# One overflow block of a mixture of experts computed on the weights of place 15, with a place table written by the routing

## The chip, the cores and the metric

The kernel runs on one core of one Trainium2 chip. The core has a matrix engine (PE, with its weight loads as PEld), a vector engine (DVE), a scalar engine (ACT), a general engine (POOL), and a sequencer for transfers (SP). Sixteen DMA engines move data between device memory and the on-chip memory. The metric is the device time of one execution in microseconds (us).

## The reference, cut to what matters

The program is one layer of a trunk: four token mixers, a cross attention, and then a mixture of experts over 512 tokens. Only the last part is touched.

```python
def _hier_moe(h, w_group, b_group, w_router, b_router, w1, w3, w2):
    g_sel = argmax(t @ w_group + b_group)            # 4 groups
    top_p, top_i = top_k(softmax(e_logits[rows, g_sel]), 2)
    expert = g_sel[:, None] * 8 + top_i              # 32 experts, two per token
    def expert_block(args):
        xb, e = args
        hid = silu(xb @ w1[e]) * (xb @ w3[e])        # 1024 -> 512
        return hid @ w2[e]                           # 512 -> 1024
    out = segment_sum(ys * slot_w[:, None], slot_tok)
```

512 tokens with two experts each make 1,024 rows, which fall on 32 experts. All is float32. The weights of one expert are three matrices of 1024x512, 6.29 MB. The reference draws its inputs from a fixed seed. Counted with its own routing they put 65 rows on expert 21 and at most 54 on any other.

## The kernel before

**Stages.** Up to about 806 us of the profiled execution the mixers and the cross attention run. Then comes the normalisation and the routing (the block from L1537), and from about 849 us the experts (the block from L1818 on each engine). The last stage adds the experts' rows to the tokens, normalises, and stores the result.

**An expert's turn.** Every expert gets one turn of up to `FIRST` = 64 rows. POOL gathers the rows from `xn_scratch` with an indirect DMA (`fetch`, L1869). PE turns them over (`e_x`, L1786), ACT copies them (`xT`). PE multiplies them by the two up matrices (`up_half`, `e_u`, L1801: 32 matmuls in two halves of 16). ACT and DVE form the hidden rows, PE turns those over (`e_h`, L1792) and multiplies them by the down matrix (`down_half`, `e_y`, L1811: 16 matmuls). ACT copies the result, and POOL scatters it to `ys_scratch` (`store`, L1876). PE does `up(q)`, then the rows of turn q+1, then the hidden rows and the down part of turn q-1.

**Weights.** An expert's weights come in six pieces of 1 MiB (n = 0 to 3 the halves of w1 and w3, n = 4 and 5 those of w2), issued by SP (`load_piece`, L1515). There are 18 slots `w_raw`, three experts' worth. `AT` gives each piece a place in the order, and its place modulo 18 is its slot. The order is (0,0..3), (1,0..3), (0,4), (0,5), (2,0..3), (1,4), (1,5) and so on: each expert's up pieces stand ahead of the down pieces of the one before. Twelve pieces are issued during the routing (`EARLY_SLOTS`) and six more as the expert block begins. From there `ring` waits for each piece until the piece that held its slot before is used (`consumed`, on `s_used`), and issues the load. SP issues strictly in this order.

**Overflow.** An expert with more than 64 rows has its rest in further blocks of 64, each an overflow job. DVE works out a table of the jobs (`jobs`, L2073 to L2086). SP writes it to device memory with a small DMA (L1823), and each engine later reads the number of jobs from there (TENSOR_LOAD). The experts run in two halves of `MID` = 16. Between them stands a loop over the jobs, on every engine. Its weights are six pieces loaded again (L1841), into slots that the order leaves open between the halves (`OVER`). The loop's rows come through `list_scratch`: POOL reads the job's row list (`ibl`, L1891), DVE makes the indices (`job_ids`), POOL gathers `xo` (L1895). At the end of each pass POOL stores the result, waits for it, and fetches list and rows of a next job, which may be empty. With the inputs above there is one job.

Of the kernel before, what the change touches and what calls it, by code (L numbers as in the profile page):

```python
# [23 lines left out]
U32 = mybir.dt.uint32  # L24
# [5 lines left out]
P = 128  # L30
# [26 lines left out]
ROUTE_CONSTS = 3 * P + EXPERTS + 3 * EXPERTS * BLOCKS + 2  # L57
# [7 lines left out]
JOBS = 16  # L65
LIST_UNIT = 16
# [36 lines left out]
def trunk(nc, a, out):  # L103
    stack = ExitStack()
    with stack:
# [1406 lines left out]
        def load_piece(sp, e, n):  # L1512
            j = AT[e, n] % DEPTH
# [13 lines left out]
        act_b, rank = (sbuf(stack, n, [P, EXPERTS * BLOCKS]) for n in ("act_b", "rank"))  # L1527
        ones_b = sbuf(stack, "ones_b", [P, EXPERTS * BLOCKS])
# [5 lines left out]
        blk_thr, blk_at, blk_e = (rc[:, r0 + EXPERTS * BLOCKS * i:r0 + EXPERTS * BLOCKS * (i + 1)] for i in range(3))  # L1534
        r0 += 3 * EXPERTS * BLOCKS
        rank1, half_no = rc[:, r0:r0 + 1], rc[:, r0 + 1:r0 + 2]
        with ExitStack() as c:  # L1537
# [6 lines left out]
            def load_gain(sp):  # L1544
# [4 lines left out]
                for j in range(EARLY_SLOTS):  # L1549
                    load_piece(sp, *ORDER[j])  # L1550
# [24 lines left out]
            idf = sbuf(c, "idf", [P, EXPERTS])  # L1575
# [150 lines left out]
        with ExitStack() as c:  # L1726
# [7 lines left out]
            ib2 = sbuf(c, "ib2", [P, 1])  # L1734
            xo, yoo = sbuf(c, "xo", [FIRST, D]), sbuf(c, "yoo", [P, FF])
# [15 lines left out]
            s_turn, o_zero = sem("o_turn"), sem("o_zero")  # L1751
            LAST = EXPERTS - 1
# [14 lines left out]

            def slot(q, n):
                return SLOT[q, n]

            def landed(eng, q, n):
                eng.wait_ge(s_raw[slot(q, n)], 16 * (len(IN_SLOT[q, n]) + 1))

            def consumed(eng, q, n):
                if q >= 0:
                    eng.wait_ge(s_used[slot(q, n)], len(IN_SLOT[q, n]) + 1)

            def y_of(t, ch):
                return raw[slot(*END[t])][:, ch * D:(ch + 1) * D]

            junk = raw[slot(*END[T])][:, 0:D]
            final_gain = raw[slot(*END[T])][:, D:2 * D]
# [36 lines left out]
            def _(sp):  # L1819
                for piece in ORDER[EARLY_SLOTS:DEPTH]:  # L1820
                    load_piece(sp, *piece)
                sp.wait_ge(s_jobs, 1)
                sp.dma_start(jobs_dram[0:1, 0:4 * (JOBS + 1)].rearrange("o (j q) -> (o j) q", q=4),  # L1823
                             jobsi[0:JOBS + 1, :]).then_inc(s_jobs_out, 16)
                def ring(pieces):
                    for e, n in pieces:
                        consumed(sp, *IN_SLOT[e, n][-1])
                        load_piece(sp, e, n)

                ring(FIRST_HALF[DEPTH:])  # L1830
                sp.wait_ge(s_jobs_out, 16)
                n = sp.value_load(jobs_dram[0:1, 2:3], min_val=0, max_val=MAX_EXTRA)
                with sp.If(n > 0):
                    for piece in FIRST_HALF[OVER_AT - DEPTH:][:PIECES]:
                        consumed(sp, *piece)
                    with sp.Fori(0, n) as r:
                        e = sp.value_load(jobs_dram[0:1, bass.ds(r * 4 + 1, 1)], min_val=0, max_val=EXPERTS - 1)
# [9 lines left out]
                for piece in END:  # L1847
                    consumed(sp, *piece)
                sp.dma_start(final_gain, bass.AP(a["rows"].tensor, 0, [[0, P], [1, D]])).then_inc(f_gain, 16)
                for b in range(2):  # L1850
                    sp.wait_ge(s_ys[b], 16 * (EXPERTS // 2))
# [10 lines left out]
            def _(pool):  # L1862
# [3 lines left out]
                def fetch(q):  # L1866
                    b = q % 2
                    wait(pool, s_tx, q - 1)
                    pool.indirect_dma_start(xs[b][:], None, xn_dram,  # L1869
                                            bass.IndirectOffsetOnAxis(idx[0:FIRST, q:q + 1], 0),  # L1870
                                            bounds_check=last_x, oob_is_err=False).then_inc(s_xs[b], 16)

                def store(q):
                    b = q % 2
                    pool.wait_ge(s_yo, q + 1)
                    pool.indirect_dma_start(ys_halves, bass.IndirectOffsetOnAxis(idy[:, q:q + 1], 0),  # L1876
                                            yo[b][:], None,
# [21 lines left out]
                for q in range(MID):  # L1899
# [3 lines left out]
                    if q == LIST_AT:  # L1903
                        pool.wait_ge(s_scattered, 16 * 2 * T)
                        pool.wait_ge(s_jobs_out, 16)
                        list_of(0)
                    if q == LIST_AT + 2:
                        pool.wait_ge(s_ids, 2)
                        pool.wait_ge(o_zero, 1)
                        rows_of_job()  # L1910
                store(MID - 1)
                n = pool.value_load(jobs_dram[0:1, 2:3], min_val=0, max_val=MAX_EXTRA)
                with pool.If(n > 0):
                    with pool.Fori(0, n) as r:
                        pool.wait_ge(o_yo, r + 1)
# [6 lines left out]
                        list_of(r + 1)  # L1922
                        pool.wait_ge(s_ids, r * 2 + 4)
                        pool.sem_inc(s_turn, 1)
                        rows_of_job()
                    pool.nop()
                pool.wait_ge(o_xs, n * 16 + 16)
                pool.sem_inc(s_turn, 1)
                for q in range(MID, EXPERTS):
                    if q + 2 < EXPERTS:  # L1930
                        fetch(q + 2)
                    if q > MID:
                        store(q - 1)
                store(LAST)
                for b in range(2):
                    pool.wait_ge(s_ys[b], 16 * (EXPERTS // 2))

            @block.tensor
            def _(pe):
# [5 lines left out]
                def up(q):  # L1945
                    pe.wait_ge(s_xT, q + 1)
                    wait(pe, s_hd, q - 1)
                    for half, (n1, n3) in enumerate(((W1A, W3A), (W1B, W3B))):
# [3 lines left out]
                        m1.then_inc(s_used[slot(q, n1)], 1)  # L1952
                        m3.then_inc(s_used[slot(q, n3)], 1)
# [6 lines left out]
                def down(q):  # L1960
                    pe.wait_ge(s_hT, q + 1)
                    wait(pe, s_yo, q - 1)
                    for half, n in enumerate((W2A, W2B)):
                        landed(pe, q, n)
                        down_half(half, q % 2, q % 2, slot(q, n)).then_inc(s_used[slot(q, n)], 1)
# [14 lines left out]
                experts(0, MID)  # L1980
                pe.wait_ge(s_jobs_out, 16)
                n = pe.value_load(jobs_dram[0:1, 2:3], min_val=0, max_val=MAX_EXTRA)
                with pe.If(n > 0):
                    pe.wait_ge(s_yo, MID)
# [21 lines left out]
                experts(MID, EXPERTS)  # L2006

            @block.scalar
            def _(act):
# [35 lines left out]
                experts(0, MID)  # L2045
                act.wait_ge(s_jobs_out, 16)
# [13 lines left out]
                experts(MID, EXPERTS)  # L2060
                consumed(act, *END[T])
# [7 lines left out]
            def _(dve):  # L2069
                do = Steps(dve, s_dve)  # L2070

                thr = blk_thr.rearrange("p (e b) -> p e b", b=BLOCKS)
# [174 lines left out]
```

## Time and profile before

| what | value |
|---|---|
| median of 3 runs | 1394.78 us (1394.43 to 1395.49) |
| the profiled execution, its own time | 1392.87 us |
| its span in the profile | 1390.9 us |
| PE busy | 1207.1 us, 87% of the span |
| DVE, ACT, POOL busy | 528.9, 407.6, 95.8 us |
| DMA, mean over the whole span | 217 GB/s |
| loads of weight pieces (`w_raw<-in_w`) | 198 (192 of the experts, 6 of the job) |

The busy shares are means over stages with different limits. From about 807 us on, the experts' weights stream in, and the rate of the DMA engines has to be read for that stretch alone.

### The profile page before, as it was taken

The numbers are of one execution on the slowest core, as the hardware profiler recorded it, in microseconds if no ns is written. First come the engines' busy times: TensorE is split into PE (matmuls) and PEld (weight loads), VectorE is DVE, ScalarE is ACT, GpSimd is POOL, SyncE is SP. The second block draws the span as 40 slices with busy tenths as digits, with TensorE's granted clock in tenths as the row PEclk, the third lists the DMA queues.
The fourth block names the chain that finished last, engine by engine and source line by source line (L and its number), as shares of the span: only waits on it lengthen the run. The fifth ranks groups of instructions, "written<-read, shape, count | busy, mean of one in ns | idle before, by whom it ended". The sixth has DMA issues, their size and how long they took to land. (4 is left out here: it accounts for less than half of the span.)

```text
span 1390.9 us, 15072 instructions
## 1 busy us (share of the span) xinstructions
PE 1207.1 (87%) x6038; PEld 795.0 (57%) x6038; DVE 528.9 (38%) x934; ACT 407.6 (29%) x674; POOL 95.8 (7%) x125
## 2 busy tenths in 40 slices
PE   6999999999999999999997854999777749977781
PEld 5887877777688787888886632333333213333330
DVE  4334464767857368555356434111000001100014
ACT  6234442444443342243153130122111101211112
POOL 2000000000000000000000003111111011111100
PEclk9999999999999999999999985999999979999996
DMA  7313213121123222423221079999999999999995
GB/s 270 116 63 105 77 63 132 49 88 57 46 70 112 76 84 91 174 91 114 100 113 61 0 310 318 374 408 405 415 417 407 426 403 402 406 414 415 407 397 196
DMA packets 50599, 301.63 MB, mean 217 GB/s; under 512 B 8985, under 2 KB 9385, under 8 KB 20451
## 3 DMA queue, kind: packets, MB, share of 16 engines
q1 hardware_dynamic: 41778, 281.06, 51.9%
q0 software_dynamic: 8224, 17.52, 3.7%
q10 hardware_dynamic: 528, 2.10, 0.4%
q8 instruction: 48, 0.79, 0.2%
q14 instruction: 21, 0.16, 0.0%
HBM read 296.77 MB, written 12.93 MB: 223 GB/s over the span
## 5 line engine op out<-in xcount | busy, mean ns | idle before, releaser
L1801 PE MATMUL e_u<-w_raw,xT 128*64 128x512 f32 x1056 | 240.4, 601 | 54.8 <-DMA w_raw<-in_w 51.3
L1801 PEld LDWEIGHTS e_u<-w_raw,xT 128*64 128x64 f32 x1056 | 80.1, 138 | 209.6 <-issue 205.5
L2092 DVE SCALAR_TENSOR_TENSOR tn<-tn,e_u 64x512 f32<-64x512 f32 x32 | 21.7, 679 | 413.3 <-ACT tn L2023 413.3
L296 DVE TENSOR_TENSOR s_lo<-s_raw,s_hi 128x2048 fp32r<-128x2048 f32 (+1 forms) x68 | 138.5, 2037 | 55.2 <-ACT s_hi L291 54.6
L291 ACT CAST s_hi<-s_raw 128x2048 fp32r<-128x2048 f32 (+1 forms) x68 | 115.9, 1704 | 110.2 <-PE pz L547 41.1
L1811 PE MATMUL e_y<-w_raw,hidT 128*64 128x512 f32 x528 | 125.1, 617 | 15.4 <-ACT hidT L2018 15.0
L515 PE MATMUL pz<-hT_hi,s_hi 128*128 128x512 f32 x288 | 116.4, 404 | 0.0
L515 PE MATMUL pz<-hT_hi,s_lo 128*128 128x512 f32 x288 | 112.7, 391 | 0.0
L515 PE MATMUL pz<-hT_lo,s_hi 128*128 128x512 f32 x288 | 112.6, 391 | 0.0
L2013 ACT COPY xT<-e_x 128x512 f32<-128x512 f32 x32 | 18.8, 586 | 312.9 <-PE e_x L1786 312.9
L531 PE MATMUL pz<-hT_hi,s_hi 128*128 128x512 f32 x256 | 102.2, 399 | 0.5
L531 PE MATMUL pz<-hT_lo,s_hi 128*128 128x512 f32 x256 | 99.7, 389 | 0.0
L531 PE MATMUL pz<-hT_hi,s_lo 128*128 128x512 f32 x256 | 99.7, 389 | 0.0
L1811 PEld LDWEIGHTS e_y<-w_raw,hidT 128*64 128x64 f32 x528 | 36.0, 140 | 79.8 <-issue 59.8
L547 PE MATMUL pz<-zR,s_hi 128*128 128x512 f32 x192 | 63.0, 389 | 0.0
L515 PEld LDWEIGHTS pz<-hT_hi,s_hi 128*128 128x128 f32 x288 | 54.4, 189 | 13.8 <-issue 3.3
L1786 PEld LDWEIGHTS e_x<-ident,xs 64*128 64x128 f32 x256 | 30.7, 200 | 53.5 <-DMA xs<-xn_scratch,idx 27.9
L515 PEld LDWEIGHTS pz<-hT_lo,s_hi 128*128 128x128 f32 x288 | 54.3, 189 | 11.8
L515 PEld LDWEIGHTS pz<-hT_hi,s_lo 128*128 128x128 f32 x288 | 54.5, 189 | 10.1
L1786 PE MATMUL e_x<-ident,xs 64*128 64x64 f32 x256 | 35.1, 279 | 28.1 <-DMA xs<-xn_scratch,idx 26.9
L1876 POOL DMA_INDIRECT ys_scratch<-yo,idy x32 | 32.2, 1006 | 377.4 <-ACT yo L2030 377.4
L948 ACT ACTIVATE tg<-pz 128x512 f32<-128x512 f32 x32 | 19.2, 598 | 125.6 <-PE pz L531 125.6
(357 smaller groups left out, 1897.0 us busy)
## 6 DMA issues: line engine op xcount, KB each, us to landing
w_raw<-in_w SPq DMA_DIRECT2D x198, 1024.0 KB, 28.0
s_raw<-in_w_mix SPq DMA_DIRECT2D x30, 1024.0 KB, 4.9
s_raw<-in_w_gb SPq DMA_DIRECT2D x32, 768.0 KB, 4.3
s_raw<-in_w_out_pieces SPq DMA_DIRECT2D x4, 1024.0 KB, 4.8
w_raw<-ys_scratch SPq DMA_DIRECT2D x8, 512.0 KB, 7.6
x_sb<-in_x SPq DMA_DIRECT2D x4, 512.0 KB, 4.9
rel_bias<-in_rel_tiles POOLq DMA_DIRECT2D x8, 256.0 KB, 3.1
decay<-in_decay POOLq DMA_DIRECT2D x8, 256.0 KB, 4.5
```

The costliest lines, as they stand in the source:

```text
L291: nc.scalar.copy(w_hi[n % 2][:, 0:w], w_raw[n % 2][:, 0:w]).then_inc(w_himade, 1)
L296: nc.vector.tensor_tensor(w_lo[n % 2][:, 0:w], w_raw[n % 2][:, 0:w], w_hi[n % 2][:, 0:w].bitcast(F32), ALU.subtract).then_inc(w_split, 1)
L515: last = nc.tensor.matmul(pz[j][:], wp, hp, start=(k == 0 and m == 0), stop=(k == KD - 1 and m == 2))
L531: last = nc.tensor.matmul(pz[0][:], wp, hp, start=(k == 0 and m == 0), stop=(k == KD - 1 and m == 2))
L547: last = nc.tensor.matmul(pz[1][:], wp, yp[:, k, :], start=(k == 0 and m == 0), stop=(k == KB - 1 and m == 2))
L948: nc.scalar.activation(tg[u % 2][:], pz[0][:], ACT.Tanh, scale=0.5).then_inc(g_tanh, 1)
L1786: last = nc.tensor.transpose(ps_x[:, k * FIRST:(k + 1) * FIRST], x[:, k::KD], ident[0:FIRST, 0:FIRST])
L1801: m = nc.tensor.matmul(ps_u[o][lo:lo + FIRST, :], xT[b][:, k * FIRST:(k + 1) * FIRST], raw[j][:, kk * FF:(kk + 1) * FF], start=k == 0, sto ...
L1811: m = nc.tensor.matmul(ps_y[o][lo:lo + FIRST, :], hT[b][:, k * FIRST:(k + 1) * FIRST], raw[j][:, kk * D + h * FF:kk * D + (h + 1) * FF], s ...
L1876: pool.indirect_dma_start(ys_halves, bass.IndirectOffsetOnAxis(idy[:, q:q + 1], 0), yo[b][:], None, bounds_check=last_y, oob_is_err=False) ...
L2013: nc.scalar.copy(xT[q % 2][:], ps_x[:]).then_inc(s_xT, 1)
L2092: nc.vector.scalar_tensor_tensor(tn[:], tn[:], 1.0, ps_u[b][0:FIRST, :], ALU.add, ALU.mult).then_inc(s_hm, 1)
```

## The change

Place 15's weights are used for two turns in a row: turn 15 for the first 64 rows, and a new turn 16 (`JOB`) for the first overflow job. There are now 33 turns. `weights_of(q)` maps a turn to a place. So that this is right for whichever expert overflows, that expert changes places with 15 (`PARTNER`). DVE writes a table `perm` of 32 entries, the expert at each place, behind the table of jobs. SP loads the weights of the places from 4 on (`FIXED` = 4) by an expert number that it reads from the table. The row indices of the places are swapped in the same way (`idx2`, `idy2`). Experts 0 to 3 are loaded before the table is there and can't be swapped: their blocks stand last in the list of jobs, and are run by the loop in the middle, as are all jobs beyond the first. If no other expert overflows, turn 16 runs on an empty list.

```diff
+            def weights_of(q):
+                return q - (q >= JOB)
...
             def consumed(eng, q, n):
-                if q >= 0:
-                    eng.wait_ge(s_used[slot(q, n)], len(IN_SLOT[q, n]) + 1)
+                if q == JOB - 1:
+                    eng.wait_ge(s_kept[n], 1)
+                elif q >= 0:
+                    freed(eng, weights_of(q), n)
+
+            def signal_of(q, n):
+                return s_kept[n] if q == JOB - 1 else s_used[slot(q, n)]
...
                 sp.wait_ge(s_jobs, 1)
                 sp.dma_start(jobs_dram[0:1, 0:4 * (JOBS + 1)].rearrange("o (j q) -> (o j) q", q=4),
                              jobsi[0:JOBS + 1, :]).then_inc(s_jobs_out, 16)
+                sp.dma_start(jobs_dram[0:1, PERM_AT:PERM_AT + EXPERTS], permi[0:1, :]).then_inc(s_jobs_out, 16)
+                sp.wait_ge(s_jobs_out, 32)
+                loaded = {q: q for q in range(FIXED)}
+
                 def ring(pieces):
-                    for e, n in pieces:
-                        consumed(sp, *IN_SLOT[e, n][-1])
-                        load_piece(sp, e, n)
+                    for q, n in pieces:
+                        if q not in loaded:
+                            loaded[q] = sp.value_load(jobs_dram[0:1, PERM_AT + q:PERM_AT + q + 1],
+                                                      min_val=0, max_val=EXPERTS - 1)
+                        freed(sp, *IN_SLOT[q, n][-1])
+                        load_piece(sp, q, n, loaded[q])
 
                 ring(FIRST_HALF[DEPTH:])
-                sp.wait_ge(s_jobs_out, 16)
...
-                for q in range(MID):
+                for q in range(JOB + 1):
                     fetch(q + 2)
...
-                experts(0, MID)
-                pe.wait_ge(s_jobs_out, 16)
+                experts(0, JOB + 1)
+                pe.wait_ge(s_jobs_out, 32)
                 n = pe.value_load(jobs_dram[0:1, 2:3], min_val=0, max_val=MAX_EXTRA)
...
-                do.after(nc.vector.tensor_copy(jobs[:, 2:3], rank[:, EXPERTS * BLOCKS - 1:EXPERTS * BLOCKS]))
+                do.after(nc.vector.tensor_scalar(jobs[:, 2:3], rank[:, JOB_BLOCKS - 1:JOB_BLOCKS], -1.0, None, ALU.add))
...
-                nc.vector.tensor_copy(jobsi[:], jobs[:]).then_inc(s_jobs, 1)
+                do.after(nc.vector.tensor_copy(jobsi[:], jobs[:]))
+
+                do.after(nc.vector.tensor_scalar(here[:], iota, e_of_job[:], None, ALU.is_equal))
+                do.after(nc.vector.tensor_scalar(gap[:], e_of_job[:], -1.0, float(PARTNER), ALU.mult, ALU.add))
+                do.after(nc.vector.scalar_tensor_tensor(perm[:], here[:], gap[:], iota, ALU.mult, ALU.add))
+                do.after(nc.vector.tensor_copy(perm[:, PARTNER:PARTNER + 1], e_of_job[:]))
+                nc.vector.tensor_copy(permi[:], perm[:]).then_inc(s_jobs, 1)
```

How the instructions stand: on SP's queue, at the start of the expert block, the kernel before has this. `jobs_scratch` is the device memory of the tables, `w_raw<-in_w` a piece of weights.

```order
20 L1515 DMA w_raw<-in_w 128x2048 x6
21 L1823 DMA jobs_scratch<-jobsi 17x4
22 L1515 DMA w_raw<-in_w 128x2048 x78
23 L1832 TENSOR_LOAD jobs_scratch
24 L1832 ISA x2
25 L1833 COMPARE_AND_BRANCH
```

The changed kernel has this in the same place.

```order
20 L1520 DMA w_raw<-in_w 128x2048 x6
21 L1845 DMA jobs_scratch<-jobsi 17x4
22 L1847 DMA jobs_scratch<-permi 1x32
23 L1520 DMA w_raw<-in_w 128x2048 x4
24 L1854 TENSOR_LOAD jobs_scratch
25 L1854 ISA x2
26 L1520 ISA
27 L1520 DMA w_raw<-in_w 128x2048 x2
28 L1520 ISA
29 L1520 DMA w_raw<-in_w 128x2048 x4
```

A second small DMA is behind the first, and from place 4 on a read of the table stands ahead of each place's first piece. The wait for both small DMAs is on the first piece of row 23.

On PE, at the end of the first half, the kernel before has this (`e_u` up, `e_h` hidden rows, `e_y` down, `e_x` rows; `xo` is the job's rows).

```order
3453 L1811 MATMUL e_y<-w_raw,hidT 64x512 x8
3454 L1801 MATMUL e_u<-w_raw,xT 64x512 x16
3455 L1792 MATMUL e_h<-ident,hd 128x64 x4
3456 L1811 MATMUL e_y<-w_raw,hidT 64x512 x8
3457 L1792 MATMUL e_h<-ident,hd 128x64 x4
3458 L1811 MATMUL e_y<-w_raw,hidT 64x512 x8
3459 L1982 TENSOR_LOAD jobs_scratch
```

The changed kernel has this.

```order
3454 L1823 MATMUL e_u<-w_raw,xT 64x512 x16
3455 L1808 MATMUL e_x<-ident,xs 128x64 x8
3456 L1814 MATMUL e_h<-ident,hd 128x64 x4
3457 L1833 MATMUL e_y<-w_raw,hidT 64x512 x8
3458 L1823 MATMUL e_u<-w_raw,xT 64x512 x16
3459 L1814 MATMUL e_h<-ident,hd 128x64 x4
3460 L1833 MATMUL e_y<-w_raw,hidT 64x512 x8
3461 L1814 MATMUL e_h<-ident,hd 128x64 x4
3462 L1833 MATMUL e_y<-w_raw,hidT 64x512 x8
3463 L2015 TENSOR_LOAD jobs_scratch
```

The rows, the up part and the down part of turn 16 stand between turn 15 and the read of the number of jobs. The loop behind that read is still there on every engine.

## Rows read from the trace of the kernel before

**Rows 1.** The page, parts 2 and 6: DMA by slice, and the weight loads (issue to landing).

```profile
DMA  7313213121123222423221079999999999999995
...
w_raw<-in_w SPq DMA_DIRECT2D x198, 1024.0 KB, 28.0
```

**Rows 2.** Stretches: start and end, length, granted TensorE clock, DMA share, GB/s.

```profile
940.00:1060.00 120.00, 1.00 1.01 412
1080.00:1100.00 20.00, 1.00 1.01 425
```

**Rows 3.** The page, part 4: the chain that ended last, by line, shares of the span.

```profile
SPq L1515 21%; PE e_u L1801 4%; DMA w_raw<-in_w 4%; PE e_y L1811 2%; DMA xs<-xn_scratch,idx 1%; DMA xo<-xn_scratch,ibx 1%; DVE x_sb L2135 1%; PE e_x L1786 1%; DMA ys_scratch<-yoo,iby 0%; DMA ibl<-list_scratch 0%; SPq L1841 0%; DVE x_sb L2129 0%; DMA w_raw<-ys_scratch 0%; PE e_h L1792 0%; POOLq L1888 0%
```

**Rows 4.** Timeline of SP, expert stage: start, length, line, operation, count.

```profile
853.56 0.31 SPq L1823 DMA_DIRECT2D jobs_scratch<-jobsi  x1
866.31 193.51 SPq L1515 DMA_DIRECT2D w_raw<-in_w  x78
1064.29 12.42 SPq L1841 DMA_DIRECT2D w_raw<-in_w  x6
1076.95 258.47 SPq L1515 DMA_DIRECT2D w_raw<-in_w  x96
```

**Rows 5.** Stretches at the start of the expert stage, columns as in rows 2.

```profile
849.00:850.00 1.00, 0.50 0.03 8
850.00:851.00 1.00, 0.50 0.93 115
851.00:852.00 1.00, 0.50 0.74 287
...
849.00:866.00 17.00, 0.51 0.96 287
866.00:877.00 11.00, 1.00 0.98 257
877.00:880.00 3.00, 1.00 0.99 356
```

**Rows 6.** SP's weight issues, 866.0 to 866.8: lengths in ns, starts, us to landing.

```profile
L1515 SPq DMA_DIRECT2D w_raw<-in_w x2: 353/529/705, 866.3 to 866.7; - x2
...
DMA to landing us min/median/max: 13.9/14.8/15.7
```

**Rows 7.** DMA queues from 845 to 885: POOL's gathers and scatters (packets, MB, share).

```profile
q0 software_dynamic: 576, 0.60, 5.4%
```

**Rows 8.** Timeline of DVE: a 32-wide operation, two 256-wide ones, turn 0's first.

```profile
848.01 0.18 DVE L1721 TENSOR_SCALAR second<-idf 128x32 f32<-128x32 f32 x1
...
851.17 0.35 DVE L2080 TENSOR_SCALAR rank<-rank,rc 128x256 f32<-128x256 f32 x1
851.56 0.48 DVE L2081 CUSTOM_DVE_ANT_0 act_b<-rank,rc 128x256 f32<-128x256 f32 x1
...
871.88 0.68 DVE L2092 SCALAR_TENSOR_TENSOR tn<-tn,e_u 64x512 f32<-64x512 f32 x1 [18.35 <-ACT tn L2023]
```

**Rows 9.** SP's table read and weight issues by line: ns min/median/max, starts.

```profile
L1832 SPq TENSOR_LOAD <-jobs_scratch x1: 712/712/712, 1059.9 to 1059.9; - x1
...
L1841 SPq DMA_DIRECT2D w_raw<-in_w x6: 362/2253/2531, 1064.3 to 1074.4; - x6
...
L1515 SPq DMA_DIRECT2D w_raw<-in_w x192: 327/2132/4704, 808.2 to 1333.3; - x192
```

**Rows 10.** Timeline of PE: turn 0's up part, turns 14 and 15, then turn 16.

```profile
859.66 10.05 PE L1801 MATMUL e_u<-w_raw,xT 128*64 128x512 f32 x32 [0.68 <-ACT xT L2013]
...
1076.17 3.65 PE L1801 MATMUL e_u<-w_raw,xT 128*64 128x512 f32 x16 [1.56 <-DMA w_raw<-in_w]
...
1080.91 3.65 PE L1811 MATMUL e_y<-w_raw,hidT 128*64 128x512 f32 x16 [0.46 <-ACT hidT L2018]
...
1112.33 7.09 PE L1801 MATMUL e_u<-w_raw,xT 128*64 128x512 f32 x32 [0.68 <-ACT xT L2013]
1119.35 1.09 PE L1786 MATMUL e_x<-ident,xs 64*128 64x64 f32 x8
```

More of the change, by code:

```diff
@@ L56 @@
 BLOCKS = 8
-ROUTE_CONSTS = 3 * P + EXPERTS + 3 * EXPERTS * BLOCKS + 2
+FIXED = 4
+PARTNER = EXPERTS // 2 - 1
+FREE_BLOCKS = (EXPERTS - FIXED) * BLOCKS
+JOB_BLOCKS = EXPERTS * BLOCKS + 1
+ROUTE_CONSTS = 3 * P + EXPERTS + 3 * JOB_BLOCKS + 2
 SMALL = 3 * KD + 8 * KB
@@ L1526, in trunk @@
         cnt = sbuf(stack, "cnt", [P, EXPERTS])
-        act_b, rank = (sbuf(stack, n, [P, EXPERTS * BLOCKS]) for n in ("act_b", "rank"))
-        ones_b = sbuf(stack, "ones_b", [P, EXPERTS * BLOCKS])
+        act_b, rank = (sbuf(stack, n, [P, JOB_BLOCKS]) for n in ("act_b", "rank"))
+        ones_b = sbuf(stack, "ones_b", [P, JOB_BLOCKS])
+        idf, idx2, idy2 = sbuf(stack, "idf", [P, EXPERTS]), *(
+            sbuf(stack, n, [P, EXPERTS], U32) for n in ("idx2", "idy2"))
         jobs, jobsi = sbuf(stack, "jobs", [P, 4]), sbuf(stack, "jobsi", [P, 4], I32)
@@ L1533, in trunk @@
         r0 += P
-        blk_thr, blk_at, blk_e = (rc[:, r0 + EXPERTS * BLOCKS * i:r0 + EXPERTS * BLOCKS * (i + 1)] for i in range(3))
-        r0 += 3 * EXPERTS * BLOCKS
+        blk_thr, blk_at, blk_e = (rc[:, r0 + JOB_BLOCKS * i:r0 + JOB_BLOCKS * (i + 1)] for i in range(3))
+        r0 += 3 * JOB_BLOCKS
         rank1, half_no = rc[:, r0:r0 + 1], rc[:, r0 + 1:r0 + 2]
@@ L1734, in trunk @@
             ib2 = sbuf(c, "ib2", [P, 1])
+            e_of_job, gap, here = (sbuf(c, n, [P, k]) for n, k in (("e_of_job", 1), ("gap", 1), ("here", EXPERTS)))
+            perm, permi = sbuf(c, "perm", [P, EXPERTS]), sbuf(c, "permi", [P, EXPERTS], I32)
             xo, yoo = sbuf(c, "xo", [FIRST, D]), sbuf(c, "yoo", [P, FF])
@@ L1750, in trunk @@
             last_x, last_y = nc.gpsimd.alloc_register("last_x"), nc.gpsimd.alloc_register("last_y")
-            s_turn, o_zero = sem("o_turn"), sem("o_zero")
-            LAST = EXPERTS - 1
+            s_turn, o_zero, s_swap = sem("o_turn"), sem("o_zero"), sem("swapped")
+            s_kept = [sem(f"kept{n}") for n in range(PIECES)]
+            JOB = MID
+            TURNS = EXPERTS + 1
+            LAST = TURNS - 1
             LIST_AT = MID // 2
@@ L1820, in _ @@
                 for piece in ORDER[EARLY_SLOTS:DEPTH]:
-                    load_piece(sp, *piece)
+                    load_piece(sp, *piece, piece[0])
                 sp.wait_ge(s_jobs, 1)
@@ L1921, in _ @@
                         pool.sem_inc(s_turn, 1)
[L1922 to L1925, printed above, removed]
                     pool.nop()
[L1927 to L1930, printed above, removed]
+                for q in range(JOB + 1, TURNS):
+                    if q + 2 < TURNS:
                         fetch(q + 2)
-                    if q > MID:
+                    if q > JOB + 1:
                         store(q - 1)
@@ L1964, in down @@
                         landed(pe, q, n)
-                        down_half(half, q % 2, q % 2, slot(q, n)).then_inc(s_used[slot(q, n)], 1)
+                        down_half(half, q % 2, q % 2, slot(q, n)).then_inc(signal_of(q, n), 1)
                 def experts(lo, hi):
@@ L2085, in _ @@
                 do.after(nc.vector.memset(jobs[:, 3:4], 0.0))
-                nc.vector.tensor_copy(jobsi[:], jobs[:]).then_inc(s_jobs, 1)
+                do.after(nc.vector.tensor_copy(jobsi[:], jobs[:]))
[4 more added lines that the diff above has]
+                nc.vector.tensor_copy(permi[:], perm[:]).then_inc(s_jobs, 1)
+                do.after(nc.vector.tensor_tensor_reduce(av[:, 0:EXPERTS], idf[:], here[:], 1.0, 0.0, ALU.mult, ALU.add,
+                                                        e_of_job[:]))
+                do.after(nc.vector.tensor_tensor(gap[:], idf[:, PARTNER:PARTNER + 1], e_of_job[:], ALU.subtract))
+                do.after(nc.vector.scalar_tensor_tensor(idf[:], here[:], gap[:], idf[:], ALU.mult, ALU.add))
+                do.after(nc.vector.tensor_copy(idf[:, PARTNER:PARTNER + 1], e_of_job[:]))
+                do.after(nc.vector.tensor_scalar(idy2[:], idf[:], 2.0, half_no, ALU.mult, ALU.add))
+                do.after(nc.vector.tensor_scalar(here[:], idf[:], float(N), -float(N), ALU.is_ge, ALU.mult))
+                nc.vector.tensor_tensor(idx2[:], idf[:], here[:], ALU.add).then_inc(s_swap, 1)
                 def experts(lo, hi):
```

113 lines of the change are left out of this document (68 added, 45 removed).

## Prediction

> **What bounds the kernel now.** I first look at the DMA row of the page. In the last third of the span, from about 860 us on, the 16 DMA engines are busy in full until the last slices [rows 1]. Averages over the whole span hide this. By stretch, the engines move 412 GB/s over 120 us of the first half and 425 GB/s where few gathers run [rows 2]. The chain that ended last says the same: its largest part is SP's issue of the weights, at 21% of the span [rows 3]. An issue on SP takes 0.33 us when nothing holds it, but 2.1 us in the median, and a piece lands 28 us after it [rows 9, 1]. One piece of 1.05 MB at 425 GB/s takes 2.47 us, so about 11 pieces are in flight and SP is held back by the full queue. PE needs 3.65 us for each half of an up part, and waits for a landing before it [rows 10]. So what ends last is the stream of 198 pieces. PE, idle for part of each turn, can take on a turn for nothing as long as the slots come free before the stream runs dry.
>
> **The change part by part.**
>
> *Six loads go.* The job's weights were six pieces between the halves [rows 4]. The inputs put 65 rows on expert 21, so there is one job, it falls to turn 16, and the loop's six loads are skipped. 6 x 1.049 = 6.29 MB. At 425 GB/s this is 14.8 us, at 412 GB/s, which has the gathers in it, 15.3 us. The gathers and the scatter of the job itself stay, and only one empty gather goes. I take 15.0 us, between the two.
>
> *DVE makes the second table.* New ahead of the signal to SP are one 257-wide comparison and one 257-wide reduction (0.35 and 0.48 us in the rows of their 256-wide kin), a reduction and four small operations in place of two (about 0.8 us together), and five 32-wide ones of 0.2 us. The sum is some 2.7 us [rows 8]. SP's small DMA stood at 853.6 [rows 4], and so moves to about 856.3, with the second one 0.4 us behind. Some seven more operations for the row indices end near 858.5. DVE's next work is at 871.9 [rows 8], so all of that is hidden.
>
> *SP waits for both tables before the ring.* This is the term that costs. In the kernel before, the ring's first pieces are issued at 866.3, as PE sets the slots free [rows 4, 6]. Now SP must first see the tables landed, and they are queued behind the six pieces issued at 849 to 852. When does the last of those land? From 849 to 866 the engines move 17 x 0.287 = 4.88 MB, to 877 another 2.83 MB, to 880 another 1.07 MB: 8.78 MB [rows 5]. Of this 0.60 MB is gathers and scatters [rows 7], so 8.2 MB are weights, and 1.9 MB of them are ring pieces. The earliest end of the six is where 6.29 + 0.6 MB are moved, at 873.8. The latest is one piece (2.5 us) ahead of the first ring piece's landing, 866.3 + 13.9 = 880.2 [rows 6], so 877.7. Give the tables 0.4 us more: the ring starts between 874.2 and 878.1. A stream starting from nothing loses 1.7 us on top: in its first 3 us after 849 it moved 0.41 MB, less the 0.3 us before the first issue, where 2.7 us at 425 GB/s are 1.15 MB [rows 5]. By 880 the ring has then moved 1.7 MB in the early case and 0.1 MB in the late one, against 1.9 MB. The lost 0.2 to 1.8 MB are 0.4 to 4.3 us of a stream that is full from there to the end, so nothing gives them back. I take 3.0 us, nearer the late end, since the landing at 880.2 is a row and the early end is only a sum of bytes. PE isn't held up: its up weights of turns 0 to 2 are among the first 18 pieces.
>
> The Trainium skill (DMA: Bandwidth & Descriptors, Anatomy of one DMA) puts about 2 us of fixed cost on a DMA, most of it the receipt of the write from the target memory. By that price, in place of my 0.4 us, the ring would start 1.6 us later, the term would be 4.6 us and the time 1384.4. No row here gives a landing of the small DMA.
>
> *SP reads the table 28 times.* One read takes 0.71 us and some register work [rows 9], about 1 us in all, per place of six pieces or 15 us. SP otherwise sits 2.1 us in each issue because the queue is full. A pause of 1 us leaves some 10 pieces in flight instead of 11: nothing, as long as SP is not the bound. The issues with an address from a register took 0.36 us at the least, as good as those with a constant [rows 9].
>
> *The turn in the middle.* Place 15's up slots come free a turn later. Turn 15's second up half starts at 1076.2 [rows 10]. Behind it in the queue are then the down pieces of places 14 and 15 and the up pieces of 16, eight pieces or 19.7 us, to 1095.9. The six slots left open in the order help only later, since they stand behind in SP's order. PE goes on with 3.65 us of up, 1.1 us of rows, 1.2 us for the hidden rows, 3.65 us of down, and half of turn 16's up part, 3.5 us [rows 10]: the first kept slots are free at 1089.3, 6.6 us before the stream would end, or 5 us with the start loss. So I cost the kept slots at nothing. If that cover were gone, each microsecond beyond it would be one of time. The loop's own waits go too, but the stream ran on at full rate beside them [rows 2], so they bring nothing.
>
> *Sum.* -15.0 + 3.0 = -12.0 us. Against the profiled execution, 1392.87 us, this is 1380.9. The median of the runs is 1.9 us above that execution, and I carry the difference over: 1394.78 - 12.0 = 1382.8 us. The case's own range, from 14.8 to 15.3 and 0.4 to 4.3, is 1379.9 to 1384.3.
>
> **The rivals.**
>
> *The tables come early (A).* If the small DMAs don't queue behind the weights, SP is back at the ring by 866 and the second term is nothing: 1379.8. For it speaks that they go to other memory and are tiny. Against it speaks that ring pieces on this queue land in the order of their issue, 14 to 16 us later with a short queue [rows 6].
>
> *The stream runs dry in the middle (B).* The cover is 5 us at full clock. Turn 0's up part took 10.05 us where the granted clock was 0.50 for most of it, against 7.09 in the middle [rows 10, 5]. If PE's clock is low around turns 15 and 16, the 9.5 us from 1079.8 to 1089.3 grow to as much as 19, the stream stands still for about 4.5 us, and the second pair of slots adds a little: some 5 us, 1387.8. Against it: the granted clock was 1.00 in 1080 to 1100 [rows 2].
>
> *SP becomes the bound, slower (C).* The 2.1 us median of an issue may be the making of a piece's transfers, and not a wait for room. Then SP has no slack, and each of the 28 reads stands in full in the stream: 28 x 1.0 = 28 us, and 1410.8. The point from which this decides is 12.0 / 28 = 0.43 us uncovered in each read. Against it: the issues of 0.33 to 0.53 us at the ring's start [rows 6, 9], when the queue was short.
>
> *The change doesn't do what it says (D).* If the expert that overflows were one of the fixed four, or had two blocks, the loop would load its six pieces as before: 1394.8 + 3.0 = 1397.8. The count of rows speaks against it.
>
> **How the numbers follow.** A measurement of this kernel can tell about 0.2%, 2.8 us, from no change. Forecast 0.66, A 0.12, B 0.14, C 0.04, D 0.02, and 0.02 for smaller sizes of B and C that end near the old time. Faster is the sum of the first three, 0.92. Same is 0.02, slower 0.06. The predicted time is the forecast's, 1382.8. The range takes in A, the forecast with the bounds of both terms, and B with something to spare: 1378.5 to 1389.0. C and D lie outside.
>
> **What would show it.** 192 weight loads in place of 198, and none from the loop. SP's first ring issue at 874 to 878 in place of 866, and a dip of the DMA rate between 870 and 880. From there on 410 to 425 GB/s without a gap, also around 1090. The read of the table on SP 28 times at 0.7 us, with the next issue shorter by about as much. DVE's chain some 2.7 us longer ahead of the first small DMA. The last expert's up part about 12 us earlier than in the kernel before, and the stage behind it unchanged. The forecast is wrong if the first ring issue is before 870 (A), if the DMA share falls near the middle (B), or if landings drift apart from 28 us down to a few while SP is the one busy (C).

## The result, and the profile after

| | time |
|---|---|
| the kernel before, same chip | 1394.61 us median (1394.40 to 1395.49, 4 runs) |
| the changed kernel | 1382.28 us median (1379.14 to 1385.35, 4 runs) |
| ratio | 0.991, 95% interval 0.9887 to 0.9933 |
| the profiled execution of the changed kernel | 1379.14 us, span 1377.2 us |

The change takes off 12.3 us where 12.0 were forecast, and 1382.28 stands beside the forecast's 1382.8. The profiled execution is the fastest of the four, so its own gain on the profiled execution before is larger, 13.7 us.

The page of the changed kernel, parts 2 and 6, with the lines that answer to [rows 1]:

```profile
DMA  7323213212123222433322059999999999999995
...
w_raw<-in_w SPq DMA_DIRECT2D x192, 1024.0 KB, 28.2
```

There are 192 loads in place of 198, and a piece still lands 28 us after its issue: the stream is full and is still the bound. The timeline of SP in the expert stage (start, length, line, operation, count), to be held against [rows 4]:

```profile
849.38 3.06 SPq L1520 DMA_DIRECT2D w_raw<-in_w  x6
857.18 0.30 SPq L1845 DMA_DIRECT2D jobs_scratch<-jobsi  x1
857.53 0.23 SPq L1847 DMA_DIRECT2D jobs_scratch<-permi  x1
876.59 445.94 SPq L1520 DMA_DIRECT2D w_raw<-in_w  x174
```

The small DMA is issued at 857.2 in place of 853.6, and the ring begins at 876.6 in place of 866.3. Between them the DMA engines run out of work. By stretch (start and end, length, granted clock, DMA share, GB/s), changed kernel:

```profile
874.00:875.00 1.00, 1.00 1.08 295
875.00:876.00 1.00, 1.00 0.57 173
876.00:877.00 1.00, 1.00 0.15 37
877.00:878.00 1.00, 1.00 1.01 115
878.00:879.00 1.00, 1.00 0.45 156
879.00:880.00 1.00, 1.00 0.96 401
...
849.00:866.00 17.00, 0.51 0.95 272
866.00:877.00 11.00, 1.00 0.87 207
877.00:880.00 3.00, 1.00 0.81 224
880.00:900.00 20.00, 1.00 1.01 417
```

Against [rows 5], 17 x 0.015 + 11 x 0.050 + 3 x 0.132 = 1.2 MB are missing by 880, 2.8 us of the stream at 425 GB/s. That is the term of 3.0 us, read from this trace.

In the middle, PE's timeline of the changed kernel shows turn 16 with no wait for a landing ahead of its up part:

```profile
1077.72 3.65 PE L1823 MATMUL e_u<-w_raw,xT 128*64 128x512 f32 x16 [1.21 <-DMA w_raw<-in_w]
...
1083.35 3.65 PE L1833 MATMUL e_y<-w_raw,hidT 128*64 128x512 f32 x16 [0.47 <-ACT hidT L2051]
1086.83 7.04 PE L1823 MATMUL e_u<-w_raw,xT 128*64 128x512 f32 x32
...
1336.40 3.65 PE L1823 MATMUL e_u<-w_raw,xT 128*64 128x512 f32 x16 [1.29 <-DMA w_raw<-in_w]
```

The first and the last of these rows give a ruler for all the kernels here. From turn 15's second up half to the last expert's it is 1336.40 - 1077.72 = 258.7 us. In the kernel before it is 1349.90 - 1076.17 = 273.7 us, the end of it from this row of the trace of before:

```profile
1349.90 3.65 PE L1801 MATMUL e_u<-w_raw,xT 128*64 128x512 f32 x16 [1.30 <-DMA w_raw<-in_w]
```

So the later part, in which the bytes of the six loads were moved, is 15.0 us shorter. The earlier part, from the issue of the six pieces to turn 15, is 228.3 us in place of 226.9. That is 1.4 us more, where the count of bytes gave 2.8. The next section shows that this earlier part differs by more than that between executions of the same code, so it can't decide between the two.

### The profile page after: what moved, and what is told of

Read it like the earlier page. It is cut to its first block and busy times, and to the rows that moved or that the text cites. A ratio compares the mean times of both kernels' runs of the same rounds, so it can differ in the third digit from the quotient of the medians.

```text
span 1377.2 us, 15337 instructions
## 1 busy us (share of the span) xinstructions
PE 1207.4 (88%) x6038; PEld 796.1 (58%) x6038; DVE 533.0 (39%) x950; ACT 407.4 (30%) x674; POOL 92.7 (7%) x122
## 5 line engine op out<-in xcount | busy, mean ns | idle before, releaser
L1823 PE MATMUL e_u<-w_raw,xT 128*64 128x512 f32 x1056 | 244.6, 609 | 61.7 <-DMA w_raw<-in_w 58.4
L1833 PE MATMUL e_y<-w_raw,hidT 128*64 128x512 f32 x528 | 120.6, 598 | 15.3 <-ACT hidT L2051 15.3
L520 PEld LDWEIGHTS pz<-hT_hi,s_hi 128*128 128x128 f32 x288 | 54.4, 189 | 13.8 <-issue 3.3
L520 PEld LDWEIGHTS pz<-hT_lo,s_hi 128*128 128x128 f32 x288 | 54.4, 189 | 11.8
L536 PEld LDWEIGHTS pz<-hT_hi,s_hi 128*128 128x128 f32 x256 | 48.1, 188 | 12.7 <-DVE s_lo L301 2.2
L513 PE MATMUL pz<-s_hi,hT_hi 128*128 128x256 f32 x192 | 55.2, 288 | 0.0
```

The costliest lines, as they stand in the source:

```text
L513: last = nc.tensor.matmul(pz[j][:, half * CW:(half + 1) * CW], hp[:, k, at:at + P], wp, start=(k == 0 and m == 0), stop=(k == KD - 1 and m ...
L520: last = nc.tensor.matmul(pz[j][:], wp, hp, start=(k == 0 and m == 0), stop=(k == KD - 1 and m == 2))
L536: last = nc.tensor.matmul(pz[0][:], wp, hp, start=(k == 0 and m == 0), stop=(k == KD - 1 and m == 2))
L1823: m = nc.tensor.matmul(ps_u[o][lo:lo + FIRST, :], xT[b][:, k * FIRST:(k + 1) * FIRST], raw[j][:, kk * FF:(kk + 1) * FF], start=k == 0, sto ...
L1833: m = nc.tensor.matmul(ps_y[o][lo:lo + FIRST, :], hT[b][:, k * FIRST:(k + 1) * FIRST], raw[j][:, kk * D + h * FF:kk * D + (h + 1) * FF], s ...
```

## The experiments

The theory: the gain is the bytes of six loads, the loss is the wait for the tables ahead of the ring, and the reads of the table and the turn in the middle cost nothing. The profiled executions give this table. "Ring" is SP's first ring issue, "early part" is from the issue of the six pieces to turn 15's second up half, "later part" from there to the last expert's second up half.

| kernel | median, us | before beside it | ratio and interval | ring at | early part | later part |
|---|---|---|---|---|---|---|
| before | 1394.61 | | | 866.3 | 226.9 | 273.7 |
| changed | 1382.28 | 1394.61 | 0.9910 (0.9887 to 0.9933) | 876.6 | 228.3 | 258.7 |
| e1, before with the wait first | 1396.65 | 1393.83 | 1.0017 (1.0008 to 1.0026) | 878.1 | 229.0 | 273.6 |
| e2, static table | 1378.46 | 1393.83 | 0.9891 (0.9876 to 0.9906) | 866.7 | 226.4 | 258.5 |
| e3, wait at the first read | 1377.99 | 1393.83 | 0.9888 (0.9873 to 0.9903) | 866.3 | 225.9 | 258.8 |
| e4, reads three times | 1382.08 | 1393.83 | 0.9915 (0.9902 to 0.9929) | 877.6 | 227.1 | 258.8 |
| f1, before without the job's loads | 1384.80 | 1396.99 | 0.9920 (0.9905 to 0.9934) | 864.2 | 229.9 | 260.8 |
| f2, 6.9 us more on PE in turn 16 | 1380.58 | 1396.99 | 0.9876 (0.9859 to 0.9894) | 866.7 | 229.5 | 259.3 |
| f3, 20.6 us more | 1393.63 | 1396.99 | 0.9980 (0.9972 to 0.9989) | 865.2 | 228.3 | 272.2 |
| f4, tables issued from ACT | 1379.21 | 1396.99 | 0.9873 (0.9859 to 0.9888) | 875.7 | 228.4 | 259.5 |
| g1, changed, again | 1382.16 | 1396.08 | 0.9901 (0.9887 to 0.9915) | 878.4 | 230.6 | 258.4 |
| g2, wait at the first read, again | 1380.28 | 1396.08 | 0.9888 (0.9873 to 0.9904) | 866.1 | 227.1 | 259.2 |
| g3, scatters late | 1382.81 | 1396.08 | 0.9908 (0.9894 to 0.9922) | 872.4 | 229.3 | 259.0 |
| g4, both | 1379.77 | 1396.08 | 0.9881 (0.9866 to 0.9896) | 866.5 | 227.6 | 259.7 |

Kernels with the same letter ran on one chip and can be compared directly. The early part differs by 2 to 3 us between runs of what is the same code (before 226.9, f1 229.9), and the later part by up to 1.3 us (258.4 in g1, 259.7 in g4). So a term of the later part is read from the ruler, to about 1 us, and one of the early part from the medians. The issue of the six pieces, the block's start, lies anywhere from 848.9 to 851.9 us. Counted from it, the ring begins 15.3 to 17.0 us later where SP doesn't wait for the tables ahead of it, and 25.2 to 28.7 us later where it does (g3: 21.0).

**e1: the new wait alone, in the kernel before.**

```diff
-                ring(FIRST_HALF[DEPTH:])
                 sp.wait_ge(s_jobs_out, 16)
+                ring(FIRST_HALF[DEPTH:])
```

> The kernel before, with one edit: SP waits for the landed table of jobs ahead of the ring and not behind its first part. Nothing else of the change is in it. Start theory (the new wait is what costs, because the small DMA stands behind six pieces): the first ring piece is issued at 874 to 878 in place of 866, and the time is 1.5 to 4 us over the kernel before, about 1397, with runs some us apart as the changed kernel's are. Rival (the small table lands early when it is alone, and only the second DMA with its 32 entries on one partition is late): first ring issue near 866, time as before, runs within 1 us.

Measured: 2.8 us over the kernel before, interval 1.1 to 3.6 us. The ring's first issue in e1, and its stretches behind the wait (the block began at 851.9 here, 2.6 us later than in the kernel before, so the ring began 26.3 us behind it in place of 17.0, and part of what these stretches lack is the later start):

```profile
856.11 0.31 SPq L1823 DMA_DIRECT2D jobs_scratch<-jobsi  x1
878.13 186.34 SPq L1515 DMA_DIRECT2D w_raw<-in_w  x78
```

```profile
866.00:877.00 11.00, 0.91 0.98 204
877.00:880.00 3.00, 1.00 0.54 86
```

The later part is unchanged at 273.6. One small DMA is late alone, so it isn't the second one with its 32 entries. The start theory holds for place and, within the interval, for size.

**e2: no wait, no reads.** The places of SP's loads are constants of these inputs. DVE still makes both tables, and SP stores them.

```diff
-                sp.wait_ge(s_jobs_out, 32)
-                loaded = {q: q for q in range(FIXED)}
+                loaded = {q: q for q in range(EXPERTS)}
+                loaded[15], loaded[21] = 21, 15
...
                 ring(FIRST_HALF[DEPTH:])
+                sp.wait_ge(s_jobs_out, 32)
```

> The changed kernel with the place table as constants of these inputs (15 and 21 exchanged): no wait ahead of the ring, no reads of the table on SP. DVE still makes the table and SP still stores it. Start theory: the whole gain of the six loads is left, 1379.5 (15.0 us under the kernel before), and the runs lie within 1 us. Rival (the spread of 6 us between runs of the changed kernel comes from its middle or from the turn on kept slots): runs still spread over several us, median near 1382.

Measured: 15.4 us under the kernel before, four runs within 1.4 us. Without the wait the whole gain of the loads is there, and nothing in the middle takes from it.

**e3: the wait moved four pieces on.** The table is read first for place 4, and four pieces of places 2 and 3 stand ahead of that.

```diff
-                sp.wait_ge(s_jobs_out, 32)
                 loaded = {q: q for q in range(FIXED)}
...
                         if q not in loaded:
+                            if len(loaded) == FIXED:
+                                sp.wait_ge(s_jobs_out, 32)
                             loaded[q] = sp.value_load(...)
```

> The changed kernel, with SP's wait for the tables moved from ahead of the ring to the first read of the table, four pieces later. The four pieces are those of places 2 and 3, which need no table. Start theory: they are issued at 866 to 870 and bridge the wait, the DMA rate doesn't fall to nothing at 876, 1380 (2 to 3 us under the changed kernel), runs closer together. Rival (reads of the table cost in the stream as well): 1381 to 1382, since the 28 reads are still there.

Measured: 15.8 us under the kernel before, level with e2. The SP timeline of e3 shows how the wait is bridged:

```profile
866.25 1.00 SPq L1520 DMA_DIRECT2D w_raw<-in_w  x2
...
869.68 1.08 SPq L1520 DMA_DIRECT2D w_raw<-in_w  x2
...
877.61 0.36 SPq L1520 DMA_DIRECT2D w_raw<-in_w  x1
```

The tables come as late as before: the fifth piece waits for them until 877.6. But the engines have four more pieces by then. Since the 28 reads are still in and e3 is level with e2, they cost nothing that the medians show.

**e4: 56 reads more.**

```diff
-                            loaded[q] = sp.value_load(...)
+                            for _ in range(3):
+                                loaded[q] = sp.value_load(...)
```

> The changed kernel with every read of the table made three times, 56 reads more at about 0.7 us each, 39 us of SP's time. Start theory with SP held back by a full queue: no change, 1382 to 1383. Rival (SP is close to being the bound, reads stand in the stream): up to 39 us more; a tenth of it, 4 us, would be seen as 1386.

Measured: 1382.08, 11.8 us under the kernel before, with a later part of 258.8, that of the changed kernel. SP's reads and issues, in the changed kernel (the first two rows) and in e4 (the last), ns min/median/max:

```profile
L1854 SPq TENSOR_LOAD <-jobs_scratch x28: 456/560/2314, 878.6 to 1301.6; - x28
...
L1520 SPq DMA_DIRECT2D w_raw<-in_w x192: 327/2053/4564, 808.4 to 1320.5; - x192
```

```profile
L1855 SPq TENSOR_LOAD <-jobs_scratch x84: 456/549/2417, 879.6 to 1304.0; - x84
```

The median issue went from 2132 [rows 9] to 2053 ns: this fits the forecast that what a read takes, the next issue waits less. The first read took 2.3 us, with four pieces issued ahead of it. Rival C falls.

**f1: the loads alone.** In the loop of the kernel before, each load is replaced by its signal.

```diff
-                            sp.dma_start(raw[OVER[n_]][:], ...).then_inc(o_raw[n_], 16)
+                            sp.sem_inc(o_raw[n_], 16)
```

> The kernel before, with the six loads of the job left out and nothing else: the job multiplies by whatever lies in its slots, so its one row is left out of the result in effect. Stream theory: 14.8 to 15.3 us off the kernel before, 1378.5 to 1379.5, all of the gain of the change comes from these bytes. Rival (the loop's waits in the middle cost too, and the turn in the changed kernel takes them away): less than 14 us, 1380 or more.

Measured: 12.2 us off, interval 9.2 to 13.3, and a later part of 260.8 in place of 273.7, 12.9 us. The stream theory's 14.8 to 15.3 doesn't hold for this kernel: the changed kernel's later part is 2.1 us shorter yet. SP stands waiting twice in the middle. What it waited for there, in f1 and then in the kernel before (us in total, times, longest):

```profile
SPq L1515 <- PE e_y L1811: 26.2, 2, 23.7
SPq L1515 <- PEq L2002: 16.6, 1, 16.6
```

```profile
SPq L1515 <- PEq L2004: 2.2, 1, 2.2
```

The wait of 16.6 us is for PE's signal at the end of the loop's pass (`o_xo`), from 1096 to 1112.5. The pieces in flight bridge it, but for a share of 0.90 from 1110 to 1115. The wait of 23.7 us, from 1133 to 1156.6, isn't bridged. The stretches of f1 (columns: length, then busy time and count of PE, PEld, DVE, ACT and POOL, granted clock, DMA share, GB/s) show where:

```profile
1140.00:1145.00 5.00, 0.00 (x0) 0.00 (x0) 0.00 (x0) 0.00 (x0) 1.90 (x2) 0.50 1.00 404
1145.00:1150.00 5.00, 0.00 (x0) 0.00 (x0) 0.00 (x0) 0.00 (x0) 0.00 (x0) 0.50 1.04 338
1150.00:1155.00 5.00, 3.69 (x18) 2.20 (x20) 1.36 (x2) 1.93 (x4) 0.00 (x0) 0.50 0.81 293
1155.00:1160.00 5.00, 5.00 (x16) 1.37 (x14) 0.00 (x0) 0.41 (x1) 0.00 (x0) 0.61 0.56 170
```

POOL gathers the next turns' rows only after the loop's last gather, PE stands still, no slots come free, and the DMA share falls to 0.56. In the kernel before PE stands still from 1130 to 1140 too, but the DMA share stays at 0.99 or more from 1130 to 1160: with the job's loads in the stream the waits were hidden. So leaving out the loads alone gives 12.9 us, and some 2 us more (1.1 to 2.4, by the spread of the ruler) come only when the job no longer runs in a loop.

**f2 and f3: how much cover the middle has.** In the static-table kernel, turn 16 makes its up part once or three times more before the one that counts.

```diff
                     wait(pe, s_hd, q - 1)
+                    if q == JOB:
+                        for _ in range(1):     # f3: range(3)
+                            for half, (n1, n3) in enumerate(((W1A, W3A), (W1B, W3B))):
+                                up_half(half, q % 2, q % 2, slot(q, n1), slot(q, n3))
```

> The static-table kernel (1378.5), in which turn 16 makes its up part once more ahead of the counting one, 6.9 us of PE's time before the first kept slot is free. By the prediction's cover of 5 to 6.6 us: 0 to 2 us over it, 1378.5 to 1380.4. If there were no cover: 1385.4. If the cover is far larger: 1378.5.

> As the one before with the up part made three times more, 20.6 us of PE's time. By a cover of 5 to 6.6 us: 14.0 to 15.6 us over the static-table kernel, 1392.5 to 1394.1. With no cover 1399.1; with a far larger one, under 1390.

The static-table kernel didn't run on this chip, so the ruler decides: later parts of 259.3 and 272.2 against e2's 258.5, 0.8 and 13.7 us more. PE's extra time is 13.90 - 7.04 = 6.9 and 27.64 - 7.04 = 20.6 us. The cover by f3 is 20.6 - 13.7 = 6.9 us, to about 1 us. The 0.8 us of f2 lie within the spread of the ruler (258.4 to 259.7), so f2 says that 6.9 us fit under the cover in full or but for 0.8. The median of f3 lies in its expected range, that of f2 0.2 us above its own. In f3 the stream stands still beside that work (timeline of PE, then the stretches):

```profile
1087.17 27.64 PE L1823 MATMUL e_u<-w_raw,xT 128*64 128x512 f32 x128
```

```profile
1095.00:1100.00 5.00, 1.00 0.32 118
1100.00:1105.00 5.00, 1.00 0.01 3
1105.00:1110.00 5.00, 1.00 0.00 0
1110.00:1115.00 5.00, 1.00 0.51 159
```

Past the cover each microsecond is one of time, and the two medians, 13.1 us apart for 13.7 us of work, say the same.

**f4: the tables on another queue.** The two small DMAs are issued by ACT, ahead of its first turn. SP still waits for them ahead of the ring.

```diff
             def _(sp):
-                sp.wait_ge(s_jobs, 1)
-                sp.dma_start(jobs_dram[...], jobsi[...]).then_inc(s_jobs_out, 16)
-                sp.dma_start(jobs_dram[...], permi[0:1, :]).then_inc(s_jobs_out, 16)
                 sp.wait_ge(s_jobs_out, 32)
...
             def _(act):
+                act.wait_ge(s_jobs, 1)
+                act.dma_start(jobs_dram[...], jobsi[...]).then_inc(s_jobs_out, 16)
+                act.dma_start(jobs_dram[...], permi[0:1, :]).then_inc(s_jobs_out, 16)
                 experts(0, JOB + 1)
```

> The changed kernel with its two small DMAs issued from ACT, so that they don't stand in SP's queue behind the six pieces. SP still waits for both ahead of the ring. Queue theory: they land within some 3 us, SP is at the ring by 866, and the time is that of the kernel without the wait, 1378 to 1379. Rival (a small DMA is late because the 16 engines are full with weights and scatters, whatever queue it is in): first ring issue at 874 or later, 1382.

The queue theory falls on its first number. Issue on ACT and SP's first ring piece:

```profile
858.32 0.49 ACTq L2075 DMA_DIRECT2D jobs_scratch<-jobsi  x1
858.84 0.23 ACTq L2077 DMA_DIRECT2D jobs_scratch<-permi  x1
...
875.73 447.55 SPq L1520 DMA_DIRECT2D w_raw<-in_w  x174
```

Nothing stands ahead of them in that queue, and they still take 17 us. Their packets are moved late too: of the 20 on this queue (q10), 7 in 861 to 866, 11 in 866 to 871, and 2 after 871.

The last of the 20 moved between 875.3 and 875.4, and the ring began at 875.7. The last of the six pieces came later yet. The sixth piece of the block in the changed kernel, and then in f4 (issue, and us to landing):

```profile
L1520 SPq DMA_DIRECT2D w_raw<-in_w x1: 506/506/506, 851.9 to 851.9; - x1
DMA to landing us min/median/max: 25.1/25.1/25.1
```

```profile
L1520 SPq DMA_DIRECT2D w_raw<-in_w x1: 504/504/504, 853.1 to 853.1; - x1
DMA to landing us min/median/max: 26.8/26.8/26.8
```

In the changed kernel it landed at 877.0, 0.4 us after the ring's start at 876.6. In f4 it landed at 879.9, 4.2 us behind it. So out of SP's queue the tables no longer land with the sixth piece, but they are far from early.

The median is nevertheless 17.8 us under the kernel before on this chip. That is the time that the queue theory gave, 1378 to 1379, and not the 1382 of its rival, although the ring began as late as the rival said. I can't say how much of it is due to the queue: the changed kernel didn't run beside it, and before itself spread from 1393.3 to 1398.9 there. f2, which doesn't wait ahead of the ring, has 1380.58 on this chip, so here the medians show no cost of the wait at all.

**g1 to g4: changed kernel, wait moved, scatters moved, both, on one chip.** The scatters are the eight DMAs by which POOL writes the row lists, 4 bytes a row.

```diff
-                for ch in range(2):
-                    for t in range(T):
-                        pool.indirect_dma_start(list_dram, ...).then_inc(s_scattered, 16)
...
                 for q in range(JOB + 1):
                     fetch(q + 2)
                     if q:
                         store(q - 1)
+                    if q == 3:
+                        for ch in range(2):
+                            for t in range(T):
+                                pool.indirect_dma_start(list_dram, ...).then_inc(s_scattered, 16)
```

> The changed kernel as it is, beside the next three on one chip. By its own earlier runs 0.991 of the kernel before.

> The kernel with SP's wait moved to the first read of the table, again, now beside the changed kernel. Start theory: 2.5 to 4 us under the changed kernel.

> The changed kernel with POOL's eight scatters of row lists moved from 853 to 864 us to the end of its fourth turn, some 45 us later; the lists are read only in the ninth. Scatter theory (their 4-byte writes slow the weights from 861 to 876, and hold the small DMAs up in whichever queue): the six pieces run at 400 GB/s or more and land by 866, the first ring piece is issued by 868, and 3 us or more are gained over the changed kernel. Rival (the slow stretch is not theirs, the gathers or the short queue make it): first ring issue still at 874 or later, time as the changed kernel's.

> Both edits together: wait at the first read, and the scatters late. Scatter theory, if the slow stretch costs the stream more than the wait does: 2 to 7 us under the kernel with the wait moved alone, since from 861 to 876 the engines moved some 235 GB/s in place of 425. If the scatters cost the stream as much at their later place: the same as with the wait moved alone.

The stretches of g1, and then those of g3:

```profile
861.00:866.00 5.00, 0.50 1.06 220
866.00:871.00 5.00, 1.00 1.31 245
871.00:876.00 5.00, 1.00 0.63 129
...
910.00:930.00 20.00, 1.00 1.02 410
```

```profile
861.00:866.00 5.00, 0.64 1.03 417
866.00:871.00 5.00, 1.00 0.98 328
871.00:876.00 5.00, 1.00 0.61 121
...
910.00:930.00 20.00, 1.00 1.01 304
```

The slow stretch is the scatters': it leaves 861 to 871 and comes up at 910 to 930, where they are now issued. There it costs 20 x 0.106 = 2.1 MB or 5 us of the stream. In g3 the ring begins 21.0 us after the six pieces' issue (851.5), in g1 28.7 us (849.8), so the tables do land earlier without them. But a dry stretch of 871 to 876 is still there, and the time is the changed kernel's. From 849 to 880 g3 moves 292 GB/s and g1 226, 2.0 MB or 4.8 us of the stream: what the start gains, the later place takes. The expectation of 3 us or more fell. g4 against g2, where SP doesn't wait ahead of the ring, shows the scatters without the dry stretch: 360, 405 and 363 GB/s from 861 to 876 without them, 246, 271 and 143 with them.

Moving the wait alone brings 1.9 us against the changed kernel on this chip (g2, expected 2.5 to 4), and 4.1 us on the other (e3 against e4). The intervals of g1 and g2 overlap, those of e3 and e4 just touch. Both edits together, g4, are level with g2: of the two outcomes expected, it is the one in which the scatters cost as much at their later place.

## Why the prediction was right, point by point

*Six loads go, -15.0.* The later part gives 15.0 and 15.3 us (changed, g1), e2 gives 15.4. The size was right: with loads and loop both gone, the stream is full on either side and is shorter by its bytes. The account of the loop was not quite: by f1, leaving out the bytes alone gives 12.9 us in the later part. The prediction said of the loop's own waits that "they bring nothing", since the stream ran on beside them. That was true of the kernel before, and only because the job's loads filled the stream meanwhile. Take the loads away and leave the loop, and some 2 us of its waits come out.

*DVE's second table, hidden but 2.7 us later.* The small DMA went from 853.6 to 857.2, 3.6 us. One operation put at 0.35 us took 1.50 us:

```profile
852.07 1.50 DVE L2119 TENSOR_SCALAR act_b<-rank 128x257 f32<-128x257 f32 x1
```

It ran while POOL cleared a tile, as an operation of 0.85 us in the same place had in the kernel before. It decided little: e1, whose small DMA is issued 4.3 us after the block's start in place of 7.8, has its ring only 0.9 us sooner after that start.

*SP waits for both tables, +3.0.* Measured 2.8 us (e1 against before, interval 1.1 to 3.6), 2.8 us from the missing bytes of the profile, 1.9 and 4.1 us from moving the wait away, and on the chip of f1 to f4 nothing. The ring began at 876.6 and 878.4 in two profiles of the changed kernel, against a forecast of 874.2 to 878.1. So e1 shows that the wait costs, and the size is known only as some 1 to 4 us. That the median came within 0.5 us of the forecast is in part luck: the four runs lie 6 us apart.

The mechanism was only half right. I put the lateness down to the tables standing behind six pieces in SP's queue. There they did land when the sixth piece did, as forecast: it landed at 877.0 in the changed kernel and at 854.1 + 19.4 = 873.5 in g3, and the ring began at 876.6 and 872.4. But f4 shows that the queue isn't what makes them late: in an empty one they took 17 us, and the ring began 25.2 us after the block's start, against 26.3 to 28.7 with the tables in SP's queue. The engines are busy with weights and with scatters meanwhile, and g3, without the scatters, has the ring 7.7 us sooner after the block's start than g1 and 6.2 us sooner than the changed kernel. Rival A fell as forecast, but the reason given for it was only part of the cause.

The Trainium skill (DMA: Bandwidth & Descriptors, Queues, rings and completion order) says that a DMA's signal is written only after every earlier write of that DMA engine, across its queues. No run here shows this: in f4 the last packet itself moved only 0.3 to 0.4 us before the ring's first issue, so the packets' own late turn is enough. What orders them so late in an empty queue stays open.

The 2 us of the Trainium skill (DMA: Bandwidth & Descriptors, Anatomy of one DMA) that the prediction weighed would have given 1384.4, an estimate. The page gives them for a DMA issued from gpsimd, and these were issued from SP. The median lies nearer to the sum without them, but the runs, 1379.1 to 1385.4, take in both. In g3 by 871 the engines had moved 6 x 0.157 + 6 x 0.355 + 5 x 0.417 + 5 x 0.328 = 6.8 MB, the six pieces with the gathers, and the ring began at 872.4, 1 to 2 us later.

*The reads, nothing.* Shown by e4: 56 more, and no change of the later part. A read took 0.56 us in the median, less than the 0.71 assumed. *The turn in the middle, nothing, with a cover of 6.6 us.* Shown by f3, 6.9 us, and f2 agrees. The 1.7 us of start loss that I took off it for caution hardly show. *The rest.* The last expert's second up half came 13.5 us earlier in the profile, where about 12 were forecast, and the stage behind it is unchanged.

The range, 1378.5 to 1389.0, was drawn wide for B, which didn't come. The runs of the changed kernel lie 6 us apart, against 1 us for the kernel before beside them, and those of e2, e3, g2 and g4, which don't wait ahead of the ring, 1.4 to 2.2 us. But f2 and f3 don't wait there either, and their runs lie 6.9 and 3.3 us apart, as wide as those of e4, f4, g1 and g3, which do (3.3 to 3.6 us). The kernel before spread over 3 to 6 us itself on the other chips, and the early part of its code differs by 2 to 3 us from run to run. Whether the wait makes the time less even stays open.

The best version is e3 (g2): 1377.99 against 1393.83, and 1380.28 against the changed kernel's 1382.16 on another chip. By its code it gives up nothing of what the change can do for other inputs, which no run here tried.

## What to carry to other kernels

Where a stream of loads is the bound, count its bytes first, and then ask at each new wait how much is left in the queue while it lasts: 6.9 us of work in the middle cost under 1 us here, and a wait for a few hundred bytes at the start cost 2 to 4 us on two chips of three. A wait for a table belongs at the first use of the table, not at the head of the loop that uses it. And what a loop hides today is hidden by what runs beside it: leave out its loads, and some of its own waits come out, 2 us here.

## What the runs showed of the hardware that I had not expected

- 1,024 writes of 4 bytes slow a stream of 8 KB packets out of proportion to their bytes. With them the engines moved 220 GB/s at a share of 1.06, without them 417 GB/s in the same 5 us.
- A DMA of a few hundred bytes issued into an empty queue took 17 us to be seen as landed (f4), although its queue moved only 20 packets, the last of them 0.3 to 0.4 us before the wait ended.
- A table read of 0.56 us on a queue whose issues wait for room is free: 84 of them in place of 28 left the later part at 258.8 us, against 258.7.
